# Turning the inverse on VectorE in place of TensorE, and masking on GpSimd, in the levels of a gated DeltaNet layer

## What is computed

```
lower = jnp.where(strict, jnp.einsum('...ik,...jk->...ij', kb, kc) * decay, 0.0)
T = lax.linalg.triangular_solve(eye + lower, eye, left_side=True, lower=True, unit_diagonal=True)
u = jnp.einsum('...ij,...jv->...iv', T, vc * bc[..., None])
w = jnp.einsum('...ij,...jk->...ik', T, kb * jnp.exp(G)[..., None])
```

## Time and profile before

| what | value |
|---|---|
| median of three runs | 2601.45 us (2599.93 to 2602.07) |
| profiled execution, first to last instruction | 2599.4 us |
| TensorE busy | 2537.5 us, 98% |
| VectorE busy | 1591.4 us, 61% |
| ScalarE busy | 951.4 us, 37% |
| GpSimd busy | 402.3 us, 15% |
| mean granted TensorE clock | 0.994 of full speed |

### The profile page before, as it was taken

The page is one execution under the profiler, slowest core; times in us unless marked ns, Lnnn a source line. Parts: engine busy times, 40 slices in busy tenths (PEclk is TensorE's granted clock), DMA queues, the critical chain, the costliest instruction groups (busy, mean ns, idle before and its releaser), DMA issues.

```text
span 2599.4 us, 53288 instructions
## 1 busy us (share of the span) xinstructions
PE 2537.5 (98%) x22828; PEld 2426.0 (93%) x22828; DVE 1591.4 (61%) x3124; ACT 951.4 (37%) x1984; POOL 402.3 (15%) x364
## 2 busy tenths in 40 slices
PE   7999999998999999999999999999999999999998
PEld 7899999997799999999999998886899999999997
DVE  6777777777775555555554734657755555555545
ACT  5544444444541222332232413446522223222322
POOL 0000000000000343234320000004103342333200
PEclk9999999998999999999999999999999999999999
DMA  4111011134511111111111324425211111111111
GB/s 147 58 52 35 27 47 47 50 129 174 178 50 41 49 50 50 50 50 50 50 49 58 113 70 131 120 75 186 76 41 50 49 50 50 50 50 50 49 41 66
DMA packets 86708, 182.49 MB, mean 70 GB/s; under 512 B 21953, under 2 KB 49913, under 8 KB 85753
## 3 DMA queue, kind: packets, MB, share of 16 engines
q1 hardware_dynamic: 77465, 166.82, 19.9%
q10 hardware_dynamic: 9008, 12.26, 1.5%
HBM read 148.02 MB, written 36.27 MB: 71 GB/s over the span
## 4 chain that ended last, share of the span: by engine, by line
PE 81%; DVE 11%; ACT 3%; issue 1%; DMA 1%; POOL 1%; ACTq 0%; DVEq 0%; POOLq 0%; SPq 0%
PE psum L2905 7%; PE psum L2903 7%; PE psum L2904 7%; PE psum L2932 6%; PE psum L2933 6%; PE psum L2934 6%; PE psum L2487 5%; PE psum L2488 5%; PE psum L2489 5%; PE psum L2561 3%; PE psum L2562 3%; PE psum L2563 3%; PE psum L2749 2%; PE psum L2513 2%; PE psum L3022 1%; PE psum L3023 1%
## 5 line engine op out<-in xcount | busy, mean ns | idle before, releaser
L2932 PE MATMUL psum<-c_hi,d_hi 128*128 128x258 f32 x1344 | 380.4, 283 | 3.4 <-DVE x_b L2084 1.7
L2933 PE MATMUL psum<-c_lo,d_hi 128*128 128x258 f32 x1344 | 379.9, 283 | 0.0
L2934 PE MATMUL psum<-c_hi,d_lo 128*128 128x258 f32 x1344 | 379.7, 282 | 0.0
L1347 POOL TENSOR_TENSOR d_lo<-d_raw,d_hi 128x1024 fp32r<-128x1024 f32 x96 | 206.9, 2178 | 609.2 <-ACT d_hi L1118 609.2
L2561 PE MATMUL psum<-x_hi,w_hi 128*128 128x352 f32 (+1 forms) x768 | 272.1, 354 | 2.6 <-DVE pre L1516 2.6
L2932 PEld LDWEIGHTS psum<-c_hi,d_hi 128*128 128x128 f32 x1344 | 254.3, 189 | 4.5 <-DVE x_b L2084 2.1
L2934 PEld LDWEIGHTS psum<-c_hi,d_lo 128*128 128x128 f32 x1344 | 254.3, 189 | 0.0
L2933 PEld LDWEIGHTS psum<-c_lo,d_hi 128*128 128x128 f32 x1344 | 253.9, 189 | 0.0
L2905 PE MATMUL psum<-x_hi_b,t_lo 128*128 128x258 f32 x896 | 253.5, 283 | 0.0
L2905 PE MATMUL psum<-x_hi,t_lo 128*128 128x258 f32 x896 | 253.5, 283 | 0.0
L2903 PE MATMUL psum<-x_hi,t_hi 128*128 128x258 f32 x896 | 252.8, 282 | 0.3 <-DVE t_lo L2060 0.3
(11 more groups left out here) (425 smaller groups left out, 6698.8 us busy)
## 6 DMA issues: line engine op xcount, KB each, us to landing
w_raw<-in_w SPq DMA_DIRECT2D x86, 512.0 KB, 3.8
t_raw<-in_w_up SPq DMA_DIRECT2D x56, 512.0 KB, 3.5
d_raw<-in_w_quad SPq DMA_DIRECT2D x48, 512.0 KB, 3.5
q_tile<-scratch_q SPq DMA_DIRECT2D x24, 256.0 KB, 3.1
scratch_att<-o_out ACTq DMA_DIRECT2D x32, 132.0 KB, 2.9
x<-in_x SPq DMA_DIRECT2D x8, 516.0 KB, 8.6
s_state<-in_s_rec_in SPq DMA_DIRECT2D x2, 2048.0 KB, 14.9
out_s_rec<-s_state SPq DMA_DIRECT2D x8, 512.0 KB, 5.9
```

Source lines behind the costliest of these rows:

```text
L1347: pool.tensor_tensor(d_lo[:, d % 3, part], d_raw[:, d % 3, part], f(d_hi[:, d % 2, part]), ALU.subtract).then_inc(sem("quad_ready"), L.add ...
L2932: mm(out, whi, uhi, start=p in (1, 5, 2) and kk == 0, stop=False, skip_group_check=True)
L2933: mm(out, whi, ulo, start=False, stop=False, skip_group_check=True)
L2934: done = mm(out, wlo, uhi, start=False, stop=kk == 1, skip_group_check=True)
```

## The change

TensorE no longer turns the inverse. VectorE does it with three 32x32 block transposes, for the first time in `front` and then behind the subtraction of levels 1 to 4. Since the blocks inside a turned inverse are at most 32 wide up to level 5, a transpose of each 32x32 block is enough. One half of each tile changes its partitions on the way (top to bottom and bottom to top), and the blocks of the second half `t` are laid out so that both matmuls of a level read and write the same places. GpSimd writes the masked diagonal blocks of levels 2 to 5 in place of VectorE. ScalarE's copy of the turned inverse goes away with the turning. The diagonal copy of the lower half becomes one instruction.

```diff
@@ ScalarE, levels
                 if level < LEVELS:
-                    act.wait_ge(sem("turned_full"), L.next("turned_full"))
-                    act.activation(turn_of(head).rearrange("p t k n -> p t (k n)"), psum[:, 5:7, 2 * P:], ACT.Copy
-                    ).then_inc(sem("turned_ready"), L.add("turned_ready"))
                     act.wait_ge(sem("prod_full"), L.next("prod_full"))
@@ GpSimd, ahead of the first MLP
+        def masked_blocks(head):
+
+            diag, step = diag_of(head), step_of(head)
+            for level in range(2, LEVELS):
+                pool.wait_ge(sem("prod_full"), L.next("prod_full"))
+                pool.tensor_tensor(eight(step), eight(diag), o3(lvl[:, level], CH), ALU.mult
+                ).then_inc(sem("blocks_ready"), L.add("blocks_ready"))
+            L.skip("prod_full", 2)
+            L.skip("blocks_ready")
+
+        L.skip("blocks_ready")
+        for head in range(HEADS):
+            masked_blocks(head)
@@ VectorE, front
-            v.tensor_copy(diag[top], low[top, :, 0:HD].rearrange("p (k t) n -> p t k n", t=2)
-            ).then_inc(sem("dve_order"), L.add("dve_order"))
-            for t_ in range(2):
-                v.tensor_copy(diag[bottom, t_], low[bottom, 1 - t_::2, HD:P]).then_inc(sem("dve_order"), L.add("dve_order"))
+            for rows, cols in ((top, slice(0, HD)), (bottom, slice(HD, P))):
+                v.tensor_copy(diag[rows], low[rows, :, cols].rearrange("p (k t) n -> p t k n", t=2)
+                ).then_inc(sem("dve_order"), L.add("dve_order"))
...
             v.tensor_tensor(eight(step), eight(diag), o3(lvl[:, 1], CH), ALU.mult
             ).then_inc(sem("blocks_ready"), L.add("blocks_ready"))
+            turned(head)
             if head == 0:
                 v.memset(inv_t[bottom, :, 0:HD], 0.0).then_inc(sem("dve_order"), L.add("dve_order"))
             skip(4, 6)
             take_product(10, head)
             take_product(11, head)
 
+        def turned(head):
+
+            inv, turn = inv_of(head), turn_of(head)
+            v.wait_ge(sem("steps_ready"), L.value("steps_ready"))
+            v.transpose(flat(turn[:, 0:1]), flat(inv[:, 0:1])).then_inc(sem("dve_order"), L.add("dve_order"))
+            v.transpose(flat(turn[top, 1:2]), flat(inv[bottom, 1:2])).then_inc(sem("dve_order"), L.add("dve_order"))
+            v.transpose(flat(turn[bottom, 1:2]), flat(inv[top, 1:2])).then_inc(sem("dve_order"), L.add("dve_order"))
+            v.wait_ge(sem("dve_order"), L.value("dve_order"))
+            v.sem_inc(sem("turned_ready"), L.add("turned_ready"))
@@ VectorE, levels
             for level in range(1, LEVELS + 1):
-                v.wait_ge(sem("prod_full"), L.next("prod_full"))
-                if level < LEVELS - 1:
-                    v.tensor_tensor(eight(step), eight(diag), o3(lvl[:, level + 1], CH), ALU.mult
-                    ).then_inc(sem("blocks_ready"), L.add("blocks_ready"))
-                if level == LEVELS:
+                if level < LEVELS:
+                    L.skip("prod_full"), L.skip("blocks_ready", level < LEVELS - 1)
+                else:
+                    v.wait_ge(sem("prod_full"), L.next("prod_full"))
...
                     v.tensor_tensor(whole_inv, whole_inv, psum[:, 5:7, 0:2 * P], ALU.subtract
                     ).then_inc(sem("steps_ready"), L.add("steps_ready"))
+                    if level < LEVELS - 1:
+                        turned(head)
@@ TensorE, quads, corners and levels
-                        done = mm(psum[out, bank + r, cols], lhs[rows, c, p], rhs(rows, c, p), start=True, stop=True,
+                        s = r ^ c
+                        done = mm(psum[out, bank + s, cols], lhs[rows, s, p], rhs[rows, s, p], start=True, stop=True,
                                   tile_position=(r * HD, c * HD))
...
-                upper, lower = inv[top, t_, p], inv[bottom, 1 - t_, p]
+                upper, lower = inv[top, t_, p], inv[bottom, t_, p]
...
                 if level < LEVELS:
-                    quads(5, 2 * P, inv, lambda rows, c, p: ident[rows, rows]).then_inc(sem("turned_full"), L.add("turned_full"))
                     pe.wait_ge(sem("blocks_ready"), L.next("blocks_ready"))
-                    quads(3, 0, step, lambda rows, c, p: inv[rows, c, p]).then_inc(sem("prod_full"), L.add("prod_full"))
+                    quads(3, 0, step, inv).then_inc(sem("prod_full"), L.add("prod_full"))
...
                     pe.wait_ge(sem("turned_ready"), L.next("turned_ready"))
-                    quads(5, 0, turn, lambda rows, c, p: prod[rows, c, p]).then_inc(sem("step_full"), L.add("step_full"))
+                    quads(5, 0, turn, prod).then_inc(sem("step_full"), L.add("step_full"))
```

## The result

The changed kernel took 2617.82 us (median of 4 runs, 2616.53 to 2622.88) against 2601.55 us before on the same chip: a ratio of **1.0068, 95% interval 1.0056 to 1.0081, so slower by 0.7%**. The profiled execution has a span of 2614.8 us, 15.4 more than before, and its own time lies 2.0 above it.

The account below looks back on a forecast made before the run. TensorE, busy 98% of the span, was taken as the bound. Per head +0.83 (level 1) and +0.47 (later steps) gave +9.1 for heads 0 to 6; the last added +5.7: +14.8, so 2616.3 us, range 2600 to 2630.

Parts of the forecast that it names:

- level 1: Each head's first level: VectorE's turn ahead of the z products delays ScalarE's product copy, +0.83 us per head.
- the last head: Final head, with sample work instead of the split on VectorE between subtractions: +5.7 us over its five levels.
- the steps S1 to S5: Times between starts of VectorE's subtraction (L1910) in levels 1 to 5: 16.54 against 16.07, +0.47 us per head.
- the stretch: Time from level 1's subtraction start in head 0 to level 5's in the last head; forecast 14.0 us longer.
- the turn: VectorE's three transposes per level, 0.43 us each, with waits and semaphore: 1.41 us of VectorE's time.
- GpSimd's mask: GpSimd's 128x512 masking of diagonal blocks, taken as 1.27 us (1.04 to 1.36); VectorE's split waits for its end.
- rival B: Levels: VectorE's split doesn't wait for GpSimd's mask; total +0.6, 2602 us, chance 0.17.
- The weight load: SP's next load, issued after the split frees its buffer: lands 3.5 us later, ScalarE waits 1.5, cover 0.6.
- the two L1765: VectorE instructions with two SBUF inputs, last head's levels 3 and 4: each meets a mask, waits about 1.1 us.
- C: Rival on VectorE's transposes: each costs 0.70 us whatever its size, 2.2 for three; 2635 us, chance 0.07.
- E: Rival: gaps in the levels lower TensorE's clock, adding 7 to 14 us; 2623 to 2630, chance 0.05.
- D: Rival: faster, 2593 us, if VectorE's subtraction-to-subtraction time stays under TensorE's 3.52 (transposes plus GpSimd wait under about 1.3); chance 0.09.

## Why the prediction was right, and where its terms were off

**The total.** 2616.3 was forecast, 2617.8 measured; slower by 0.6% forecast, 0.7% measured. Of its three terms level 1 was nearly right, the last head right in sum and not in its parts, and the steps S1 to S5 too large; 3.1 us outside the stretch made up for that, so the closeness of the total is in part luck.

**Level 1, +0.83 per head: 0.93 to 0.96 measured in five heads, 1.31 in head 3, and its mechanism shown** by the run that moves ScalarE's wait. The mis-sized term is the turn: it holds VectorE for 1.53 (from 244.27 to the z product at 245.80), not 1.41. The three transposes are 0.44 each, 0.47 apart, as estimated, but the wait and the semaphore behind them take 0.15, not 0.05 (and the forecast's 1.36 for the three is 1.35 when added up). The same 0.1 makes the step from S4 to S5 3.71 in place of 3.60. From level 1's own mask (L1872, now L1881) to S1 it took 3.51 before and 4.56 after, alike in heads 1 to 6 (the mask itself comes some 0.1 sooner, forecast 0.08), and in head 0 4.28 and 5.20. So head 0 lost 0.92 as well, though its S1 is only 0.08 later: its mask began 0.84 earlier in this execution. And what made head 3 dearer isn't level 1 but lies ahead of it: VectorE stood idle for 0.50 before an L1654 at 313.21, where the same place of head 2 has 0.14; the cause is open.

**S1 to S5, +0.47 per head: +0.17 in head 2, +0.5 in all seven.** The mis-sized term is GpSimd's mask: 1.17, where I took 1.27 from L1407; 1.04 was the lower end. With the first split ending 0.55, not 0.60, behind it, each of the three steps with a mask is 0.13 or 0.14 shorter than forecast. Also, before's steps weren't the same in all heads: head 1's four took 16.41 and head 6's 16.34, where the changed kernel has 16.23 and 16.25. That the split waits, the doubt of rival B, is settled by the first split's 1.23 against 0.75. The weight load came as said: ScalarE waited 1.31 for it in level 3, forecast 1.5, and nothing waited for ScalarE; it waited 1.22 once more in level 4, which the forecast left out.

**The last head, +5.7: +0.6 in level 1 and +5.2 in its four steps, 5.7 in all, but not by its terms, so the sum is luck.** They were 0.8, 0.9, 0.8, 1.8 and 1.4; measured are 0.6, 1.0, 1.35, 1.3 and 1.6. Of the two L1765 that I had wait 1.1 each on a mask, one waited 0.40 and one not at all. They are L1775 now, in levels 3 and 4 (VectorE and GpSimd):

```profile
645.77 1.17 POOL L1370 TENSOR_TENSOR pair<-pair,lvl 128x512 f32<-128x512 f32 x1 [5.68 <-PE psum L2771]
646.39 1.62 DVE L1775 TENSOR_TENSOR x_lo<-o_in,x_hi 128x1024 fp32r<-128x1024 f32 x1 [0.50 <-ACT x_hi L975]
...
652.71 1.23 DVE L1775 TENSOR_TENSOR x_lo<-o_in,x_hi 128x1024 fp32r<-128x1024 f32 x1
652.78 2.17 POOL L1370 TENSOR_TENSOR pair<-pair,lvl 128x512 f32<-128x512 f32 x1 [5.85 <-PE psum L2771]
```

In level 3 ScalarE's own half (L975) came 0.50 late, when the mask was half over; in level 4 VectorE began 0.07 ahead of GpSimd, and it was GpSimd that waited.

**Outside, 0 forecast, +3.1 measured.** No run shows that the change made it. The rest of the span, outside the stretch, lay between 2030.1 and 2036.7 in the ten profiled executions, and the kernel before with one wait moved has the largest value. In the changed kernel 2.5 of the 3.1 come after the start of a round trip through memory ahead of the attention: in the chain of waits the write of q took 3.55 (second line) where it took 2.60 before (first line), and after it TensorE's clock was lower (table by stretch; 1.00 before, from 1580 to 1590):

```profile
1572.80 2.60 DMA scratch_q<-q_wide
```

```profile
1585.63 3.55 DMA scratch_q<-q_wide
```

```profile
1593.00:1605.00 12.00, 11.11 (x95) 10.03 (x96) 7.23 (x37) 9.00 (x35) 0.00 (x0) 0.86 0.41 129
```

The write took 3.55 or 3.56 in three more runs as well (the wait moved, the mask beside the turn, both), and 2.60 or 2.61 in the six others; what decides it is open. The clock was lower at this place in runs with the short write too (0.88 over 14 us with the masks alone moved) and 1.00 in runs with the long one (the wait moved), so it doesn't follow from the write.

So the forecast of the stretch was high by 1.7 (14.0, which is 14.8 less head 0's 0.83, against 12.3), and the outside hid it: the steps were 2.8 less than forecast, level 1 of heads 1 to 6 was 1.0 more.

**The rivals.** B falls by the split of 1.23. C falls by 0.44 for each transpose. E falls where it charged its price: the granted clock was 1.00 over the levels of heads 1, 2 and 3, gaps and all. Only the last head, at the lower clock for part of its levels already before, lost some: 0.50 from S2 to S3, before 0.63, and 0.67 from S3 to S4, before 0.84 (tables by stretch, S3 to S4, before and after):

```profile
640.91:651.86 10.95, 8.37 (x126) 4.87 (x126) 7.11 (x11) 1.09 (x2) 0.00 (x0) 0.84 0.85 351
```

```profile
650.45:662.66 12.21, 9.35 (x94) 4.88 (x92) 7.91 (x13) 0.60 (x1) 2.17 (x1) 0.67 0.54 223
```

So part of the last head's +5.2 may be clock, which the forecast had at nothing there; how much was not measured.

D is wrong for this kernel. It named the right place, VectorE's stretch from one L1910 to the next, but its limit of 1.3 per step for turn and wait was too strict: that is what it takes to reach TensorE's 3.52, while any step under before's 4.03 gains. With the wait for GpSimd gone, the level 1 wait moved and the last head left on TensorE, a turn of about 1.4 and steps of 3.59 make the kernel faster than before.

## What to carry to other kernels

Work that moves from a full engine to one with idle time pays only if it goes in behind what others wait for on that engine: here one ScalarE wait, standing earlier than its first use, cost 7.8 us, and a mask that met a split another 7.6, which together is more than the change lost in the stretch (12.3). Before giving an elementwise product to GpSimd, look at which VectorE instructions with two SBUF inputs run in that moment, and start it beside one-input work. In the head without cover (the last one) keep what was there.

## What the runs showed of the hardware that I had not expected

The wait between the two engines goes both ways: GpSimd's mask, 1.17 elsewhere, took 2.17 where VectorE's L1775 had begun 0.07 earlier, and L1775 kept its 1.23. GpSimd's spans are rough, but the 1.00 more is near the 1.16 that were left of L1775. It came again in the run with the last head's turn on TensorE (VectorE's line is L1783 there, GpSimd's L1380):

```profile
626.83 1.22 DVE L1783 TENSOR_TENSOR x_lo<-o_in,x_hi 128x1024 fp32r<-128x1024 f32 x1
```

```profile
626.99 2.07 POOL L1380 TENSOR_TENSOR dec<-pair,lvl 128x512 f32<-128x512 f32 x1 [4.53 <-DVE pair L1938]
```

The mask is 0.91 longer with 1.06 of L1783 left. The page "SBUF — State Buffer" of the Trainium skill (SBUF: two separate sides) says that of a GpSimd instruction and a VectorE one with two SBUF inputs whichever starts first has the shared ports for its whole instruction and the other blocks; these rows agree, and so does the first split's 1.23.

VectorE's transposes cost the same with a change of partition halves (64x256) as without (128x256), 0.44 each, and a running GpSimd didn't lengthen them: beside the mask their means over heads 1 to 6 are 444, 440 and 439 ns.

In the ten profiled executions the same code at the start reached S1 of head 0 between 91.5 and 98.5 us, though no edit touched what lies more than some 10 us ahead of it. Two single spans of this kernel can therefore differ by some us without a cause in the edit; a stretch can be read more closely, to about 1 us (the steps of heads 0 to 6 took 113.2 in the kernel before and 113.8 with its one wait moved).
